# Up weights a pass ahead, GpSimd's sums behind VectorE's PSUM sums, and transfers moved at the seams

## The reference

```python
h = rms_norm(x, ffn_pre_g[l]) * (1.0 + scale2) + shift2
u = depthwise_conv_centred(h @ w_up[l], conv_w[l], conv_b[l])   # 1024 -> 2 * 2816, width 3
a, bval = jnp.split(u, 2, axis=-1)
y = (jax.nn.gelu(a, approximate=True) * bval) @ w_down[l]        # 2816 -> 1024
x = x + gate2 * rms_norm(y, ffn_post_g[l])
```

## Time and profile before

| | |
|---|---|
| median of 3 runs | 3242.9 us |
| the profiled execution | 3244.99 us |
| its span, first to last instruction | 3243.2 us |
| mean granted clock of TensorE | 0.982 of 2.4 GHz |
| up passes 0 to 21 | about 1756 to 2242 us |
| down groups of the first half | 2245 to 2467 us |
| up passes 22 to 43 | 2468 to 2940 us |
| down groups of the second half | 2944 to 3234 us |

### The profile page before, as it was taken

One profiled execution on the slowest core, in us unless ns is written; L12 is line 12 of the kernel. 1 busy time (PEld: TensorE's weight loads), 2 busy tenths in 40 slices (PEclk: granted clock), 3 DMA queues, 4 the chain that ended last, 5 costly groups with the idle time before them and its releaser, 6 DMA issues. The chain is left out here.

```text
span 3243.2 us, 35529 instructions
## 1 busy us (share of the span) xinstructions
PE 3069.8 (95%) x13529; PEld 2457.1 (76%) x13529; DVE 2248.2 (69%) x2298; ACT 1448.0 (45%) x1848; POOL 540.8 (17%) x512
## 2 busy tenths in 40 slices
PE   7999999999999999999998899999999999897998
PEld 7777777777788888778887777777788777776887
DVE  5678777783799999976666666766555676665444
ACT  4433111113899999933333433333443333333432
POOL 0011441341000000000002232331202223320000
PEclk8999999999999999999999999999999999998999
DMA  8634233216411211376653222224662222225664
GB/s 321 215 141 141 109 108 110 85 62 223 120 33 37 54 38 33 89 219 209 209 202 141 85 78 78 67 70 138 211 209 99 78 68 70 78 79 174 209 207 135
DMA packets 153050, 408.12 MB, mean 126 GB/s; under 512 B 17288, under 2 KB 37768, under 8 KB 148392
## 3 DMA queue, kind: packets, MB, share of 16 engines
q1 hardware_dynamic: 135424, 353.92, 34.0%
q0 software_dynamic: 9968, 35.13, 2.9%
q10 hardware_dynamic: 7488, 16.78, 1.3%
HBM read 296.51 MB, written 104.02 MB: 123 GB/s over the span
## 5 line engine op out<-in xcount | busy, mean ns | idle before, releaser
L90 PE MATMUL second_ps_a<-up_in_hi,up_wu_hi 128*128 128x512 f32 x728 | 289.9, 398 | 42.7 <-DVE ffn_u L2743 20.8
L1525 DVE TENSOR_TENSOR att_prob_lo<-att_prob,att_prob_hi 128x1024 fp32r<-128x1024 f32 x256 | 309.7, 1220 | 24.3 <-ACT att_prob_hi L1484 23.1
L91 PE MATMUL second_ps_a<-up_in_lo,up_wu_hi 128*128 128x512 f32 x728 | 286.1, 393 | 0.0
L92 PE MATMUL second_ps_a<-up_in_hi,up_wu_lo 128*128 128x512 f32 x728 | 286.0, 393 | 0.0
L2795 DVE TENSOR_TENSOR ffn_wd_lo<-ffn_wd_st,ffn_wd_hi 128x1024 fp32r<-128x1024 f32 x110 | 130.5, 1223 | 218.2 <-ACT ffn_wd_hi L2646 218.2
L1484 ACT ACTIVATE att_prob_hi<-att_prob 128x1024 fp32r<-128x1024 f32 x256 | 272.3, 1064 | 0.0
L1478 ACT ACTIVATE att_prob<-att_ps_s 128x1024 f32<-128x1024 f32 x256 | 262.6, 1026 | 7.8 <-PE att_ps_s L1592 7.7
L90 PE MATMUL second_ps_b<-up_in_hi,up_wu_hi 128*128 128x512 f32 x504 | 202.7, 402 | 38.0 <-DVE up_wu_lo L2330 22.0
L2330 DVE TENSOR_TENSOR up_wu_lo<-up_w_st,up_wu_hi 128x1024 fp32r<-128x1024 f32 x88 | 88.9, 1010 | 200.3 <-ACT up_wu_hi L2323 200.3
L2646 ACT ACTIVATE ffn_wd_hi<-ffn_wd_st 128x1024 fp32r<-128x1024 f32 x110 | 110.9, 1051 | 249.5 <-PE second_ps_a L92 114.9
L2323 ACT ACTIVATE up_wu_hi<-up_w_st 128x1024 fp32r<-128x1024 f32 x88 | 73.7, 837 | 330.0 <-DMA up_w_st<-in_w_up 324.1
(11 more groups left out here) (339 smaller groups left out, 8259.1 us busy)
## 6 DMA issues: line engine op xcount, KB each, us to landing
ffn_wd_st<-in_w_dn SPq DMA_DIRECT2D x110, 512.0 KB, 4.7
up_w_st<-in_w_up SPq DMA_DIRECT2D x88, 512.0 KB, 4.9
ffn_g_raw<-scratch_g SPq DMA_DIRECT2D x88, 192.0 KB, 4.2
scratch_gates<-proj_out SPq DMA_DIRECT2D x64, 256.0 KB, 2.0
early_w_st<-in_w_branch SPq DMA_DIRECT2D x32, 512.0 KB, 5.9
merge_gate<-scratch_gates SPq DMA_DIRECT2D x64, 256.0 KB, 3.3
scratch_g<-ffn_g SPq DMA_DIRECT2D x22, 512.5 KB, 6.1
scratch_g<-ffn_g SPq DMA_DIRECT2D x21, 511.5 KB, 6.1
```

What stands on the lines that cost most here:

```text
L90: pe.matmul(out, w_hi, x_hi, start=first, stop=False)
L91: pe.matmul(out, w_hi, x_lo, start=False, stop=False)
L92: return pe.matmul(out, w_lo, x_hi, start=False, stop=last)
L1525: dve.tensor_tensor(prob_lo[:, s % LAG, :], prob[:, s % RING, :], prob_hi[:, s % LAG, :], ALU.subtract)\
```

## The change

- **Places.** The place of the up weights holds A11, A12 and A21 only. A22 has a place of its own for even passes and one for odd ones.
- **Loads.** Three transfers in place of two. Weight i is loaded when the sums of weight i-1 are made, low A of i-1 is made and low LAST of i-2 is made. So it is issued a pass earlier than before. Weight 23 waits for the last down product of the first half.
- **GpSimd.** The sums S1, S2 of weight i+1 wait for U2 of pass i, S3, S4 for U3 of pass i.
- **Split.** High and low of S34 move from pass i-1 to pass i: ScalarE makes the high part at the head of the pass, VectorE the low part behind the convolutions. LAST goes behind gelu and behind `times`. VectorE takes C11 before low A, and C12 before low S12.
- **Seams.** The first down weights wait for less. The last g of a half is stored by GpSimd's queue (with a semaphore of its own). The gate rows are loaded behind the third group's transfers, and only the norm of the first tile of a half waits for them. The x1 loads wait until two down groups are done. The pieces of h come two groups later.

```diff
-        self.st = at("w_st", [P, 2, D], 0, F32)
+        self.st = at("w_st", [P, 3, BLK], 0, F32)
+        self.a22 = [at(f"w_a22_{v}", [P, 1, BLK], a * kib, F32) for v, a in enumerate((6, 54))]
@@ load
         if i == NP:
             sp.wait_ge(self.s_dlo, 2 * NP - 2)
         elif i:
-            sp.wait_ge(self.s_lo, self.GROUPS * i)
-        sp.dma_start(self.st[:, 0, :], self.w_up[2 * (i % NP)]).then_inc(self.s_w, 16)
-        sp.dma_start(self.st[:, 1, :], self.w_up[2 * (i % NP) + 1]).then_inc(self.s_w, 16)
+            sp.wait_ge(self.s_sum, 4 * i)
+            sp.wait_ge(self.s_lo, self.GROUPS * (i - 1) + self.A + 1)
+        if i >= 2:
+            sp.wait_ge(self.s_lo, self.GROUPS * (i - 1))
+        if i == NP + 1:
+            sp.wait_ge(self.s_dn, NP // 2 * 7)
+        c = 2 * (i % NP)
+        sp.dma_start(self.st[:, 0:2, :], self.w_up[c].rearrange("p (c q) -> p c q", q=BLK)).then_inc(self.s_w, 16)
+        sp.dma_start(self.st[:, 2, :], self.w_up[c + 1][:, 0:BLK]).then_inc(self.s_w, 16)
+        sp.dma_start(self.a22[i % 2][:, 0, :], self.w_up[c + 1][:, BLK:D]).then_inc(self.s_w, 16)
...
+    def wait_all_g(engine, half):
+        for v in range(2):
+            engine.wait_ge(s_gst[v], 16 * gst_before(v, half + 1))
+        engine.wait_ge(s_gst_last, 16 * (half + 1))
@@ sync: load_dn
             if m - 2 * first_group(half) < 2:
-                sp.wait_ge(wu.s_lo, wu.GROUPS * NP * (half + 1))
+                sp.wait_ge(wu.s_sum, 4 * NP * (half + 1))
+                sp.wait_ge(wu.s_lo, wu.GROUPS * (NP * (half + 1) - 1) + wu.A + 1)
+                sp.wait_ge(wu.s_lo, wu.GROUPS * (NP * (half + 1) - 1))
@@ sync: load_g
-            for a in range(2):
-                sp.wait_ge(s_gst[a], 16 * ((NP // 2) * half + gr + 1))
+            if gr == GR - 1:
+                wait_all_g(sp, half)
+            else:
+                for a in range(2):
+                    sp.wait_ge(s_gst[a], 16 * (gst_before(a, half) + gr + 1))
@@ sync: end of a half
-            store_g(last)
-            sp.wait_ge(wu.s_lo, wu.GROUPS * NP * (half + 1))
-            sp.dma_start(g2[:], gate_rows).then_inc(s_g2, 16)
...
+                if k == 2:
+                    sp.wait_ge(wu.s_lo, wu.GROUPS * NP * (half + 1))
+                    sp.dma_start(g2[:], gate_rows).then_inc(s_g2, 16)
-                if half == 0 and k % 2 and k < 2 * KH:
-                    if k == 1:
+                if half == 0 and k % 2 and 2 < k < 2 * KH + 2:
+                    if k == 3:
+                        wait_all_g(sp, half)
...
-                    th.load_piece(sp, (k + 1) // 2)
+                    th.load_piece(sp, k // 2)
@@ gpsimd
-                    for o in wu.SUMS:
+                    pool.wait_ge(s_u2, i + 1)
+                    for o in (wu.S1, wu.S2):
                         wu.add(pool, i + 1, o)
-            pool.wait_ge(s_g, NP * (half + 1))
+                    pool.wait_ge(s_u3, i + 1)
+                    for o in (wu.S3, wu.S4):
+                        wu.add(pool, i + 1, o)
+            store_g(pool, NP * (half + 1) - 1, s_gst_last)
+            pool.wait_ge(s_dn, down_done(first_group(half) + 2))
@@ scalar: pass_of
             if c:
-                wu.high(act, i, wu.LAST)
+                wu.high(act, i, wu.S34)
                 tap(i - 1, 1)
             copy_p1(i)
             if c:
                 gelu(i - 1)
+                wu.high(act, i, wu.LAST)
...
-                for g in (wu.A, wu.S12, wu.S34):
+                for g in (wu.A, wu.S12):
@@ vector: pass_of
                 convolve(i - 1, 1)
+                wu.low(dve, i, wu.S34)
+                times(i - 1)
                 wu.low(dve, i, wu.LAST)
-                times(i - 1)
...
+            take_c11(i)
             if more:
                 wu.low(dve, i + 1, wu.A)
             else:
                 low_dn(2 * n)
-            take_c11(i)
             take_u3(i)
             take_c22(i)
-            if more:
-                wu.low(dve, i + 1, wu.S12)
-            else:
+            if not more:
                 low_dn(2 * n + 1)
             take_c12(i)
             if more:
-                wu.low(dve, i + 1, wu.S34)
+                wu.low(dve, i + 1, wu.S12)
```

More of the change, by code:

```diff
@@ L2293, in source @@
             return self.own[:, at:at + 2, :]
-        return self.st[:, 1:2, BLK:2 * BLK] if g == self.LAST else self.sums[:, self.SLOTS_OF[g], :]
+        return self.a22[i % 2][:] if g == self.LAST else self.sums[:, self.SLOTS_OF[g], :]
     def add(self, pool, i, o):
@@ L2449, in g_at, with gst_before, store_g @@
         return g_first if i == 0 else g_ring[i % 2]
-    def sync(sp):
-        def store_g(i):
-            half, c, v = i // NP, i % NP, i % 2
-            first, to = (1, 0) if half == 0 else (0, HALF - 1)
-            many = HALF - first if half == 0 else NCV
-            sp.wait_ge(s_g, i + 1)
-            sp.dma_start(g_d[c, :, to:to + many], g_at(i)[:, first:first + many]).then_inc(s_gst[v], 16)
+    def gst_before(v, half):
+        return half * (NP // 2 - v)
+    def wait_all_g(engine, half):
+        for v in range(2):
+            engine.wait_ge(s_gst[v], 16 * gst_before(v, half + 1))
+        engine.wait_ge(s_gst_last, 16 * (half + 1))
+    def store_g(engine, i, stored):
+        half, c = i // NP, i % NP
+        first, to = (1, 0) if half == 0 else (0, HALF - 1)
+        many = HALF - first if half == 0 else NCV
+        engine.wait_ge(s_g, i + 1)
+        engine.dma_start(g_d[c, :, to:to + many], g_at(i)[:, first:first + many]).then_inc(stored, 16)
+    def sync(sp):
         def load_dn(m):
@@ L2706, in scalar @@
                         wu.high(act, NP, g)
-                if half == 0 and k % 2 == 0 and 0 < k <= 2 * KH:
+                if half == 0 and k % 2 == 0 and 2 < k <= 2 * KH + 2:
                     for o in range(th.MANY):
-                        th.high(act, k // 2, o)
+                        th.high(act, k // 2 - 1, o)
                 if n % GR == GR - 1:
@@ L2782, in times @@
             elif i >= 3:
-                dve.wait_ge(s_gst[i % 2], 16 * (i // 2))
+                half, c = divmod(i, NP)
+                if i % NP == 1 and half:
+                    dve.wait_ge(s_gst_last, 16)
+                else:
+                    dve.wait_ge(s_gst[i % 2], 16 * (gst_before(i % 2, half) + c // 2))
             if i in (NP, NP + 1):
@@ L2802, in norm_tile @@
             wide = g2[:].rearrange("p (c q) -> p c q", q=BLK)
+            if t in (0, LAST_TILE[0] + 1):
+                dve.wait_ge(s_g2, 16 * (2 if t else 1))
             if t < NT - 1:
@@ L2885, in vector @@
                         wu.low(dve, NP, g)
-                if half == 0 and k % 2 == 0 and 0 < k <= 2 * KH:
+                if half == 0 and k % 2 == 0 and 2 < k <= 2 * KH + 2:
                     for o in range(th.MANY):
-                        th.low(dve, k // 2, o)
+                        th.low(dve, k // 2 - 1, o)
                 if n % GR == GR - 1:
```

27 lines of the change are left out of this document (12 added, 15 removed).

## The result

The changed kernel takes 3130.58 us (median of 4 runs, 3129.03 to 3133.86), the kernel before, on the same chip, 3243.59 (4 runs, 3241.47 to 3246.50): ratio 0.9652, 95% interval [0.9636, 0.9669], faster by 113 us. The forecast was 3122, its range 3110 to 3156. The profiled execution has a span of 3127.2 us against 3243.2, so 116.0 us are to be accounted for.

What follows compares the result with a forecast made beforehand. TensorE, 95% busy, was taken to follow a serial 21.6 us ring through the up-weight load. 45.5 + 51.7 + 1.1 + 12.4 + 10.6 = 121.3 off the 3242.9 median gave 3121.6, stated as 3122, range 3110 to 3156.

Steps and rivals of the forecast that it cites:

- The ring, and its end: Up passes: a serial ring through the weight load sets 21.6 us; opened, passes fall to 19.05, gaining 45.5 and 51.7 us.
- Hold and split cost and gain nothing: Up passes: holding GpSimd's sums and moving S3, S4 a pass later cost nothing as long as 3.7 us of cover hold.
- The first passes, 1.1 us: First passes: GpSimd's first sum no longer delays a low part taking 3.37 us against 2.29; gain 1.1, bounds 0 and 1.5.
- The first seam, 12.4 us: First up-to-down seam: third group starts 9.8 us earlier, plus 2.6 after the old gap; sum 12.4, bounds 0 and 14.
- The second seam, 10.6 us: Second up-to-down seam: third group ready at T+45 instead of 55.6 behind pass 43; gain 10.6, bounds 0 and 16.6.
- x1 behind the third group: Seams: x1 loads moved away, with store and gate rows, let the third group's data land earlier; no size of its own.
- The store by GpSimd, 0.4 us at most: Seams: storing the last g from GpSimd's queue costs 0.4 us at most by the row, an estimated 2.5 by the page.
- Nothing left out, 98: Upper bound on both halves' pass gains together; with 0.5 us of stall left in each of 37 passes, 78.
- the lower end of the range: 3110 us, said to be both seams at their upper bounds and 0.4 in the first passes.
- the rival of passes in part: Up passes: a late load or late S3, S4 leaves 1 us in each of 37 passes; 3159 us, chance 0.20.

## Why the prediction was right, and where it was not

- **The ring, and its end.** Right: 45.9 and 52.0 us for 45.5 and 51.7. That the load's wait made the ring is shown from both sides, by the run with only the loads (passes 19.04) and the one with all but the early load (21.2 and 21.5). That one lies above my 20.7 in the main because the weights take 6.2 us to be there and not 5.2.
- **Hold and split cost and gain nothing.** Right (3127.69 and 3131.04 against 3130.58). The cost of GpSimd's sums beside VectorE was right in kind: 1.3 us alone, 2.1 in the way of one.
- **The first passes, 1.1 us.** Mis-sized, and for another reason than mine: 4.5 us gained in pass 1, 0.5 lost in pass 0. The low part that I expected to come back from 3.37 us did (2.28), and pass 0 was no shorter for it. In pass 1, gaps of 3.34, 0.53 and 2.92 us stood before at the transposes, after, 3.00, 0.58 and 0.53; from the last gap of before to the end of the pass, 13.9 us, TensorE's granted clock is 0.88, where after it is 1.00 in the last 9.6 us. Before, the 1 MB load of the next weights went out beside ScalarE's stores of h, and ScalarE stood 3.84 us for one of them to land. After, that load goes out at 1780.08, ahead of those stores, and ScalarE's longest such wait is 1.39 us. The run with only the loads has the short pass 1, and the one with the late load has the long wait again (5.08 us, load at 1793.45), so the early load brought it. The two rows of before:

```profile
1794.05 0.33 SPq L2279 DMA_DIRECT2D up_w_st<-in_w_up  x1
...
1800.45 0.78 ACT L1843 ACTIVATE ffn_h_staged<-second_ps_b,keep_mod 128x512 f32<-128x512 f32 x1 [3.84 <-DMA scratch_h<-ffn_h_staged]
```

- **The first seam, 12.4 us.** The step that failed. Its sum up to the third group holds (9.7 us; 9.8 predicted), and the clock's share behind the old gap came as well, but 8.3 us were lost at groups 10 and 11. The prediction moved the pieces of h by two groups and asked only which transfers they would meet, not what their high and low parts would stand in front of in ScalarE's and VectorE's lists. The run with the pieces a group sooner gives 8.0 back. With those 8.0, the seam would have gained 11.9.
- **The second seam, 10.6 us.** Sized right where it was worked out: 11.4 us at the third group. A further 4.6 us were lost in groups 34 and 35. That boundary costs 2.4 to 7.6 us over ten kernels in two clusters, with the kernel before profiled once, in the lower one, and its sibling with only the loads in the upper one, so I count this as no cost of the change; one profile each doesn't prove it. That the x1 loads beside the rows of g make the stall was shown by taking them away twice. What decides between the clusters in one execution stays open.
- **x1 behind the third group.** The prediction counted this among what brings the rows early. It is worth 3.9 us at the second half's third group and nothing at the first's; whether it is worth anything over the whole, one profile each can't tell (3132.29 against 3130.58, intervals overlapping).
- **The store by GpSimd, 0.4 us at most.** Right: 0.56 us to issue, and SyncE's way is no faster.
- **Slips in the working.** "Nothing left out, 98" should be 97.2 (45.5 and 51.7). The terms named for the lower end of the range (1.6 and 6.0 us in the seams, 0.4 in the first passes) give 3114 and not 3110, and the rival of passes in part stands at 3159, outside a range said to hold most of it. None of this decides whether 3130.58 lies inside.
- **The start, 3.8 us that no step had.** Pass 0 starts at 1751.4 us before (the table ahead of the prediction has "about 1756") and at 1744.8 to 1749.3 in the thirteen profiles with any part of the change; no edit touches that stretch but the first up loads' form, and the thirteen spread over 4.5 us themselves. With one profile of the kernel before, what these 3.8 us are stays open.

The sum was 5.3 us too large on the span (121.3 against 116.0). That it came so near is in part luck, since terms of opposite sign met: 8.5 and 4.1 short in the seams, 2.9 and 3.8 over at the start and 0.7 in the passes.

## What to carry to other kernels

When a step of a helper's work is moved to a later slot, look up what is queued right behind that slot on every engine that takes part, at the last of its repeats above all: here the fourth of four pieces landed ahead of a block's norm and took back 8 of 12 us. When a ring is named, follow it to the one wait that closes it; opening that one gave all the passes' gain, and the hold and the split added nothing to it. Judge a gain of a few us at the place that it was meant for, group by group, since another place in the same trace may swing by as much from one execution to the next; and transfers that aren't needed for a whole block are best held until the ones that are needed next have landed.

## What was not expected of the hardware

GpSimd and VectorE cost each other more than GpSimd's small share on the page suggests: without the hold, 303 us of passes carry 123.3 us of GpSimd for 82.3, and 281.9 us of VectorE for 238.0, with the same instructions. A stall of the same kind at the same place of the program came in two sizes, 2.4 to 2.9 us and 5.5 to 7.6, in ten kernels whose instructions and issue times there are the same but for an x1 load or two.
